# The opening of a one-core encoder layer: the first pair of modulation weights loaded ahead of the first two weight units, and its first dot placed between the variance and the root

## The reference

```python
x = _layernorm(x, ln_in_g, ln_in_b)
c_act = jax.nn.silu(c)
mod = (c_act @ w_ada[l] + b_ada[l]).reshape(B, N_SUBLAYERS, 3, D)
shift, scale, gate = mod[:, :, 0], mod[:, :, 1], mod[:, :, 2]
h = x * (1.0 + scale[:, 0, None, :]) + shift[:, 0, None, :]
y = _swiglu(h, ffn1_w_in[l], ffn1_w_out[l])
x = _layernorm(ALPHA * x + 0.5 * gate[:, 0, None, :] * y, post_ln_g[l, 0], post_ln_b[l, 0])
```

## Time and profile before

| | us |
|---|---|
| median of 3 runs | 954.46 (954.41 to 955.03) |
| the profiled execution | 954.59 |
| its span | 952.8 |
| TensorE matmul busy | 938.2 (98% of the span) |
| VectorE busy | 506.4 (53%) |
| ScalarE busy | 374.1 (39%) |
| GpSimd busy | 267.6 (28%) |
| DMA, mean over the span | 134 GB/s |

### The profile page before, as it was taken

One profiled execution on the slowest core, in us unless ns is written; L12 is line 12 of the kernel. 1 busy time (PEld: TensorE's weight loads), 2 busy tenths in 40 slices (PEclk: granted clock), 3 DMA queues, 4 the chain that ended last, 5 costly groups with the idle time before them and its releaser, 6 DMA issues.

```text
span 952.8 us, 10887 instructions
## 1 busy us (share of the span) xinstructions
PE 938.2 (98%) x4233; PEld 757.7 (80%) x4233; DVE 506.4 (53%) x713; ACT 374.1 (39%) x567; POOL 267.6 (28%) x222
## 2 busy tenths in 40 slices
PE   8999999999999999999999999999999999999997
PEld 5788888888888888788767687888888888888886
DVE  6956767455464855777666488632232322233334
ACT  6752232232322313664586456532322323221224
POOL 0021111111105412337844575611111111125125
PEclk9999999999999999999999999999999999999999
DMA  9836565656644663122411121333223232213302
GB/s 359 364 131 201 185 209 181 200 175 211 198 152 143 224 226 113 70 89 89 133 66 45 45 69 66 111 111 108 91 93 107 89 98 95 83 64 120 119 20 88
DMA packets 38563, 127.21 MB, mean 134 GB/s; under 512 B 4080, under 2 KB 6256, under 8 KB 38512
## 3 DMA queue, kind: packets, MB, share of 16 engines
q1 hardware_dynamic: 38512, 126.52, 39.6%
HBM read 123.36 MB, written 2.10 MB: 132 GB/s over the span
## 4 chain that ended last, share of the span: by engine, by line
PE 92%; DVE 3%; POOL 1%; ACT 1%; DMA 1%; issue 1%; SPq 1%; POOLq 0%; DVEq 0%; ACTq 0%
PE bank L601 28%; PE bank L603 28%; PE bank L602 28%; PE bank L957 1%; PE bank L981 1%; DMA ada_first<-ada_w 1%; PE bank L968 1%; PE bank L686 1%; PE bank L687 1%; PE bank L680 1%; POOL cq L2015 0%; DVE w_lo L1081 0%; SPq L509 0%; DVE lat L1535 0%; PE bank L727 0%
## 5 line engine op out<-in xcount | busy, mean ns | idle before, releaser
L1081 DVE TENSOR_TENSOR w_lo<-raw,w_hi 128x1024 fp32r<-128x1024 f32 x153 | 206.2, 1355 | 278.4 <-ACT w_hi L1053 278.0
L601 PE MATMUL bank<-h_hi,w_hi 128*128 128x512 f32 x727 | 284.5, 391 | 0.0
L603 PE MATMUL bank<-h_hi,w_lo 128*128 128x512 f32 x727 | 283.0, 389 | 0.0
L602 PE MATMUL bank<-h_lo,w_hi 128*128 128x512 f32 x727 | 282.9, 389 | 0.0
L1053 ACT ACTIVATE w_hi<-raw 128x1024 fp32r<-128x1024 f32 x153 | 155.8, 1031 | 189.7 <-PE bank L603 188.2
L1917 POOL TENSOR_TENSOR a_lo<-act_t,a_hi 128x512 fp32r<-128x512 f32 x44 | 59.0, 1340 | 420.1 <-ACT a_hi L1175 420.1
L603 PEld LDWEIGHTS bank<-h_hi,w_lo 128*128 128x128 f32 x727 | 136.5, 188 | 28.6
L601 PEld LDWEIGHTS bank<-h_hi,w_hi 128*128 128x128 f32 x727 | 136.5, 188 | 28.4 <-issue 0.5
L602 PEld LDWEIGHTS bank<-h_lo,w_hi 128*128 128x128 f32 x727 | 136.6, 188 | 27.9
L601 PE MATMUL bank<-a_hi,w_hi 128*128 128x512 f32 (+1 forms) x374 | 141.2, 377 | 0.0
L602 PE MATMUL bank<-a_lo,w_hi 128*128 128x512 f32 (+1 forms) x374 | 140.8, 377 | 0.0
(11 more groups left out here) (304 smaller groups left out, 1044.6 us busy)
## 6 DMA issues: line engine op xcount, KB each, us to landing
raw<-wunits SPq DMA_DIRECT2D x145, 512.0 KB, 3.2
ada_ring<-ada_w SPq DMA_DIRECT2D x56, 512.0 KB, 4.3
ada_first<-ada_w SPq DMA_DIRECT2D x16, 512.0 KB, 11.0
raw<-wunits SPq DMA_DIRECT2D x16, 384.0 KB, 2.9
x<-xT SPq DMA_DIRECT2D x8, 256.0 KB, 5.1
outT<-x SPq DMA_DIRECT2D x8, 256.0 KB, 2.6
K<-k_rope SPq DMA_DIRECT2D x2, 512.0 KB, 8.1
c_act<-c_rows SPq DMA_DIRECT2D x1, 512.0 KB, 6.4
```

The lines of the kernel that those rows point to most:

```text
L601: mm(out, lh, rh, start=first, stop=False)
L602: mm(out, lh, rl, start=False, stop=False)
L603: return mm(out, ll, rh, start=False, stop=last)
L1081: nc.vector.tensor_tensor(lo, raw[:, slot, 0:width], hi.bitcast(F32), SUB).then_inc(s_lo, 1)
```

## The change

SP issues `ada_pair(0)` ahead of `unit(0)` and `unit(1)`. The body of the dot becomes a function, `first_dot`; the first dot of pair 0 is issued by VectorE right after `tvar`, ahead of the wait for ScalarE's guess and the four root steps, and the wait for `c_act` moves up with it. The second dot of pair 0 and all others stay where they were.

```diff
+            ada_pair(0)
             unit(0)
             unit(1)
-            ada_pair(0)
             ada_pair(1)
...
             rt(ts(tvar[:], meanvar[:, :, 1], LN_EPS, None, ADD))
+            def first_dot(k, i):
+
+                a = 2 * k + i
+                dve.wait_ge(s_ada1[a % FIRST_RING], 16 * (a // FIRST_RING + 1))
+                if a >= 2:
+                    dve.wait_ge(s_adadone, a - 1)
+                stt(junks[a % 2], ada_first[:, a % FIRST_RING, :], 1.0, c_act[:], MUL, MUL,
+                    accum_out=mod_pair[:, k, i:i + 1]).then_inc(s_adadone, 1)
+
+            dve.wait_ge(s_cact, 1)
+            first_dot(0, 0)
             dve.wait_ge(s_tq, 1)
...
             assert nroot[0] == ROOT_STEPS
-            dve.wait_ge(s_cact, 1)
...
             for k in range(KD):
-                for i in range(2):
-                    a = 2 * k + i
-                    dve.wait_ge(s_ada1[a % FIRST_RING], 16 * (a // FIRST_RING + 1))
-                    if a >= 2:
-                        dve.wait_ge(s_adadone, a - 1)
-                    stt(junks[a % 2], ada_first[:, a % FIRST_RING, :], 1.0, c_act[:], MUL, MUL,
-                        accum_out=mod_pair[:, k, i:i + 1]).then_inc(s_adadone, 1)
+                for i in range(2) if k else (1,):
+                    first_dot(k, i)
```

## The result

| | before | with the change |
|---|---|---|
| median, us | 954.49 (954.01 to 955.41, 22 runs) | 955.88 (955.03 to 956.27, 22 runs) |
| profiled execution, us | 954.59 | 955.77 |
| its span, us | 952.8 | 954.0 |
| ratio | 1 | 1.0013, 95% interval 1.0007 to 1.0019 |

The change costs 1.4 us, 0.13%. By the bound of 0.2% that is "no change", but the interval lies clear of 1: it is a small loss, of the size that was forecast (955.8). In microseconds the interval is +0.7 to +1.8.

The account below looks back on a forecast made before the run. TensorE-bound from 28.8 us on, so the third activation tile's start decides; ScalarE's wait for units adds 1.49 us, 0.14 comes back: 954.46 + 1.35 = 955.8 us, "no change" on its slow side; range 954.3 to 957.0.

Parts of the forecast that it names:

- Places kept, contents exchanged: SP's saturated row of loads: pair 0 lands at 12.66 and 13.92, unit 0 at 15.14, unit 1 at 16.33.
- 1.44 to 1.54 us late: ScalarE waits for units 0 and 1, so the first normalisation starts at 17.31 to 17.41 instead of 15.87.
- its cover: VectorE's tshift comes at 15.6 instead of 14.93, its reader at 17.3: 1.7 us of cover, delay costed at nothing.
- The lead that it wins: VectorE gains 0.8 us, then lags about 1.0 us waiting for ScalarE's split of unit 2, at no further cost.
- the 0.14 us that ScalarE gets back: ScalarE's slack at 22.82, waiting for VectorE until 22.96, comes back as VectorE is earlier: -0.14 us.
- the aside: VectorE's dot ahead of the root steps without the moved loads: tshift would have 0.27 us of cover, still enough.
- The sum: +1.49 - 0.14 = +1.35 us at TensorE's matmul of 28.85, the start of the third activation tile.
- That rival: TensorE's clock falls to 1.2 GHz after longer pauses, 3.1 us on top, 958.9 us; chance 0.06.
- The first rival: The lead survives: units 0 and 1 still in time for ScalarE, only VectorE's lead left, 954.3 us; chance 0.07.
- the second: The change is free: ScalarE's row behind x_tok has slack, its waits shrink, 954.5 to 955.2 us; chance 0.08.
- The fourth: The exchanged loads take 1.5 us each, not 1.2; unit 1 lands at 16.9, time 956.4 us; chance 0.06.

Follow-up runs that it names:

- the halves: Two runs against the kernel before: only pair 0's loads moved ahead of units 0 and 1, +1.11 us; only the first dot moved, +1.18 us.
- dose: The changed kernel with loads ordered unit 0, pair 0's first tile, unit 1, second tile: +0.32 us on before; with pairs 0 and 1 ahead of the units: +3.54.
- loads alone: The kernel before with only pair 0's loads moved ahead of units 0 and 1, the dot left behind the root steps: 955.53 us.
- no warming matmuls: The changed kernel without the warming matmuls behind the statistics of x (0 and 0 instead of 7 and 1): 955.72 us.
- the dot alone: The kernel before with only the first dot moved ahead of the root steps, the loads in their old order: 955.60 us.
- normalisations first: The changed kernel with ScalarE doing the four normalisations ahead of the splits of units 0 and 1: 955.96 us.

## Why the prediction was right

**The loads.** Places kept, contents exchanged: right to 0.1 us. With the 0.42 of offset, unit 0 was expected at 14.72 and unit 1 at 15.91, and they landed at 14.79 and 15.97. The bandwidth rule of the Trainium skill (DMA: Bandwidth & Descriptors, Specifications), which would have put unit 1 half a microsecond later, does not describe this stretch: the rows show 414 to 424 GB/s where the page has 358, which it gets by dividing a stack's bandwidth between two cores.

**ScalarE.** `x_tok` was to start 1.44 to 1.54 us late. It started 1.12 late, 1.54 with the offset taken off. The offset itself is 0.35 us by the landings of the two units and 0.52 by `tvar`, so this is 1.5 to 1.6. The mechanism was tested by the halves and by dose; taken away, the wait moved to another engine and the loss stayed.

**VectorE.** The dot was free, and `tshift` had its cover. The lead that it wins and the wait for unit 2's split in which it is lost (1.5 foretold, 1.52 measured) came as worked out, but for the 0.47 us that it waits for `act_t` of the first tile, which was not foretold. So did the 0.14 us that ScalarE gets back: `act_t` of the second tile follows the split of unit 2 after 0.95 us with no wait before it.

What was wrong is the aside that the dot could also stand there without the moved loads: that costs +1.18, because the dot waits 1.64 us for its weights.

**The sum.** +1.35, measured +1.39 in the medians. In the profiles the third tile is 1.09 later, 1.51 with the offset: 1.54 - 0.14 and the 0.15 of the slower transposes, less a few hundredths. The 0.15 was no term of the sum; that the medians come within 0.04 us of it is in part luck, as their interval is +0.7 to +1.8.

**The clock.** Here the prediction was wrong twice, and the errors did not touch the sum. It said 1.00 throughout, and the clock fell in the profiled execution. That rival had its event, and the rule that the Trainium skill states (TensorE: Matmul & The Clock Gate, Part 1), that idleness brings the throttle back, agrees with this trace, where the fall came behind the pause of 1.58 us; with the loads alone a pause of 1.41 kept the clock. But its price, 3.1 us, was wrong: the step that failed is "they cost 3.1 us on top". It doubled all 3.75 us of matmuls in front of the third tile and set 0.6 us of waiting against them. In the changed kernel the clock was back before that piece began (23 against 25.62 us). Where it did reach into the piece, it was back before the three `h_lo` matmuls and took 1.05 to 1.2 us, and TensorE's room there is 1.0 us by the starts, not 0.6. What came through was 0.0 to 0.2 us.

**The first rival**, that units would be in time in any place, fell with the idle times of 1.21 and 0.18 us. So did the second, that the change is free: the wait before `h_hi` grew to 0.57 us and did not shrink. The fourth, longer loads, fell with the landings.

**What stays open.** Whole change +1.39, loads alone +1.11, no warming matmuls +1.28: the differences are within the intervals, and I don't explain them. Nor do I know why the clock falls in one execution and not in the next.

## What to carry to other kernels

In a saturated row of loads a place is worth a fixed time, here 1.2 us for 512 KB. Moving a load forward is paid by those that it passes, so ask of each of them who waits for it and how long its cover is. Where three engines and the loads run level to 0.2 us, as here, moving one thing earlier only changes the name of the one that is waited for; the start of the first stretch that is bound without a pause is the number to follow. And an instruction put into a hole needs its data by the start of the hole, or everything behind it waits too.

## What the runs showed of the hardware

- The granted clock of the same kernel fell in one execution and not in another, with the same pause of 1.26 to 1.27 us on TensorE ahead of it. In the kernels with a pause of 1.3 to 1.6 us before the transposes it fell in two profiles (the change, 1.58; the dot alone, 1.32) and stayed in one (loads alone, 1.41). The kernel before has it too: of 95 executions beside the experiments 12 have a mean granted clock of 0.996 (954.71 us on average), the others 0.998 or 0.999 (954.49).
- The opening's first 14 us shift by up to 1.0 us between executions (`tvar` from 12.61 to 13.58), while the 362.4 us behind the third tile repeat to 0.2 us over all profiles, and to 0.1 wherever TensorE waited or was just in time at that tile.
- One profile (normalisations first) reports a granted clock of 0.95 over its whole span, though its 443 matmuls from 100 to 200 us are as many as in the others.
